# Expert outputs added into one row per token by the scatter, and the last norms' roots taken for three and for two tiles together

## The chip, the cores and the metric

The kernel runs on one core of one Trainium2 chip. Its five engines work side by side and wait for each other by semaphores: TensorE (PE; its weight loads are PEld), VectorE (DVE), ScalarE (ACT), GpSimd (POOL) and SyncE (SP), which only issues transfers. Sixteen DMA engines move the data; SyncE's transfers stand in the profile as queue q1 (hardware), GpSimd's as q0 (software). The metric is the device time of one execution in microseconds.

## The reference, cut to what matters

One trunk layer is computed for 128 context tokens and 512 latent tokens: 640 tokens of 1024 numbers, five tiles of 128 tokens. After both attentions and the first norm comes the part that the change touches:

```python
def hier_moe(h, ...):                       # 16 experts: top-1 group of 4, top-2 expert in it
    ...
    for e in range(N_EXPERTS):
        gg, uu = jnp.split(t @ w_gate_up[e], 2, axis=-1)
        out = out + combine[:, e:e + 1] * ((jax.nn.silu(gg) * uu) @ w_down[e])
    return out.reshape(b, s, d)

x = ln_affine(DEEPNORM_ALPHA * x + g2 * hier_moe(h, ...), ln2_g, ln2_b)
```

Only two of the 16 weights `combine` of a token are not zero. So there are 640 x 2 = 1280 pairs of token and expert, and each token's output is the sum of two rows. All numbers are float32, and each matmul is done in three passes over high and low parts of its operands.

## The kernel before, in words

**Order of the whole.** The kernel is one block with a program for each engine, written out by hand. The stages follow each other: projections (0 to 484 us), attention, branches and output projection with the first norm, routing, the expert loop (about 1085 to 1440 us), the last norm.

**Routing.** The pairs are laid into slots, 128 to a tile, with whole tiles for each expert; here 19 tiles are used. `words` holds three words for each pair: the row to be written (expert choice times 640 plus token), the token and the weight. VectorE forms `tile_words` (L1412 to L1415) and `at_place` (L1417), TensorE turns them into a table of slots (L1753), and VectorE writes that to `table` (L1463, L1464). A slot without a pair keeps the number 4096 (`NOBODY`), which lies above the bound of both indirect transfers, so that such a row is not moved.

**Expert loop.** For each tile, GpSimd gathers 128 rows of `h2_scr` into `xs`, TensorE turns them and computes gate, up (24 matmuls each) and down (24), ScalarE and VectorE split weights and activations in high and low parts. Weights land in three places of four chunks of 0.5 MB (`w_raw`, `raw_b`, `raw_c`). SyncE loads a chunk as soon as VectorE has split the former one in its place (`expert_in`, L760), so a chunk is issued almost a full turn of its place before it is used. ScalarE scales the output to `yo` (`take_out`, L965). GpSimd's `store_rows` then does in order: copy of the addresses and gather for tile + 3, scatter of `yo` to `pair_scr` (L1981), wait for that scatter, copy of the next addresses (L1985). When all is stored it signals `moe_over`.

**Last norm.** SyncE waits for `moe_over` and loads two rows for each token, `ya` and `yc` (L776, L777). VectorE: `combine` adds them, multiplies by the gate and adds the residual, with the row's sum (L1494 to L1498); `root_z` computes 1/sqrt of one tile's variance by `rsqrt_column` (10 small operations); `gain_z` multiplies by the gain (L1509). ScalarE: `square_z` and `norm_z`. The loop over tiles has combine, gain of two tiles before, root of the tile before. GpSimd stores each tile with a DMA that adds to the output (L2003), which SyncE set to the bias at the start (L700).

**Around the new transfers.** At about 41 us SyncE issues the bias copies, then loads projection weights block by block. After the last block before the attention (a block of `w_br_b`) it waits for the end of the projections (`pj_ready`) and then loads the second attention bundle. The first attention bundle is loaded by GpSimd, near the end of the projections, with the stores of the gate rows around it (L411 to L422, L1833).

## Time and profile before

| | us |
|---|---|
| median of 3 runs | 1500.85 (1499.09 to 1501.25) |
| the profiled execution | 1499.63 |
| its span | 1497.4 |
| TensorE busy | 1300.7 (87% of the span) |
| VectorE busy | 989.6 (66%) |
| ScalarE busy | 649.3 (43%) |
| GpSimd busy | 171.7 (11%) |

All times are microseconds from the span's start unless marked ns. "Idle before <- releaser" is the time in which the engine had nothing to do and what ended it. A share of the transfer engines is the time that packets took, over that of 16 engines; where two queues' packets overlap in time it can be a little over one. "To landing" runs from the issue of a transfer to its semaphore.

### The profile page before, as it was taken

How to read it: one execution, taken by the hardware profiler on the slowest of the kernel's cores; microseconds unless marked ns; L12 is line 12 of the kernel's file. 1: busy time of each engine (PE TensorE's matmuls, PEld its weight loads, DVE VectorE, ACT ScalarE, POOL GpSimd, SP SyncE). 2: the span in 40 equal slices, each digit the busy share in tenths (PEclk: the TensorE clock that was granted, in tenths of full speed). 3: DMA queues.
4: the chain of work that ended last, by engine and by line, in shares of the span. 5: the costliest groups of instructions: out<-in, count | busy, mean ns of one | idle time of the engine just before them, and what ended most of it. 6: DMA issues, size and time to landing. Idle time of an engine off the chain costs nothing.

```text
span 1497.4 us, 20859 instructions
## 1 busy us (share of the span) xinstructions
PE 1300.7 (87%) x6836; PEld 1063.8 (71%) x6836; DVE 989.6 (66%) x1814; ACT 649.3 (43%) x962; POOL 171.7 (11%) x236
## 2 busy tenths in 40 slices
PE   6899999999999778799986799996389999999940
PEld 3677777667887667788886688785368888888830
DVE  3655521838561777755555844499689999999936
ACT  2422222323222566545553322200357888888812
POOL 0012111111122000000000000100101121112201
PEclk9799999999999899999998799997589999999975
DMA  9856554453535676602202434436489999999834
GB/s 354 268 183 218 190 211 162 155 183 102 183 134 172 160 181 173 172 26 61 80 19 69 160 121 137 146 137 243 166 301 354 364 383 388 391 391 375 312 149 70
DMA packets 144419, 301.05 MB, mean 201 GB/s; under 512 B 18972, under 2 KB 24636, under 8 KB 144344
## 3 DMA queue, kind: packets, MB, share of 16 engines
q1 hardware_dynamic: 122104, 232.19, 45.1%
q0 software_dynamic: 20800, 62.63, 13.1%
q10 hardware_dynamic: 1440, 5.24, 1.1%
q8 instruction: 45, 0.74, 0.2%
q14 instruction: 30, 0.25, 0.1%
HBM read 258.69 MB, written 53.90 MB: 209 GB/s over the span
## 4 chain that ended last, share of the span: by engine, by line
PE 73%; DVE 14%; issue 6%; ACT 4%; DMA 2%; SPq 1%; POOL 0%; ACTq 0%; DVEq 0%; POOLq 0%
PE psum_pair L1556 7%; PE psum_pair L1557 7%; PE psum_pair L1558 7%; PE psum_pair L1777 5%; PE psum_pair L1778 5%; PE psum_pair L1779 5%; PE psum_pair L1695 4%; PE psum_pair L1643 4%; PE psum_pair L1696 4%; PE psum_pair L1697 4%; PE psum_pair L1656 4%; PE psum_pair L1633 4%; PE psum_pair L1792 2%; PE psum_pair L1793 2%; PE psum_pair L1794 2%
## 5 line engine op out<-in xcount | busy, mean ns | idle before, releaser
L1556 PE MATMUL psum_pair<-w_parts,h_hi 128*128 128x512 f32 x520 | 209.9, 404 | 6.3 <-DVE h_lo L1164 6.3
L1557 PE MATMUL psum_pair<-w_parts,h_hi 128*128 128x512 f32 x520 | 205.5, 395 | 0.0
L1558 PE MATMUL psum_pair<-w_parts,h_lo 128*128 128x512 f32 x520 | 205.4, 395 | 0.0
L1186 DVE TENSOR_REDUCE minus_max<-psum_pair 128x1 f32<-128x640 f32 (+1 forms) x160 | 114.3, 715 | 99.0 <-PE psum_pair L1633 98.6
L874 ACT ACTIVATE p_unnormed<-psum_pair,minus_max 128x640 f32<-128x640 f32 (+1 forms) x160 | 113.5, 709 | 144.4 <-DVE minus_max L1186 144.2
L1022 DVE TENSOR_TENSOR w_parts<-w_raw,w_parts 128x1024 fp32r<-128x1024 f32 x72 | 83.3, 1220 | 106.1 <-ACT w_parts L789 106.0
L1633 PE MATMUL psum_pair<-k_bundle,q_bundle 128*128 128x512 f32 (+1 forms) x576 | 128.4, 342 | 5.8 <-ACT p_unnormed L874 5.1
L1656 PE MATMUL psum_pair<-v_bundle,p_turned 128*128 128x64 f32 (+1 forms) x1008 | 131.3, 275 | 0.0
L1556 PEld LDWEIGHTS psum_pair<-w_parts,h_hi 128*128 128x128 f32 x520 | 99.2, 191 | 37.4 <-issue 18.3
L1656 PEld LDWEIGHTS psum_pair<-v_bundle,p_turned 128*128 128x128 f32 x1008 | 122.9, 193 | 1.4
L1558 PEld LDWEIGHTS psum_pair<-w_parts,h_lo 128*128 128x128 f32 x520 | 99.3, 191 | 21.5
L1557 PEld LDWEIGHTS psum_pair<-w_parts,h_hi 128*128 128x128 f32 x520 | 99.5, 191 | 19.0
L1633 PEld LDWEIGHTS psum_pair<-k_bundle,q_bundle 128*128 128x128 f32 x576 | 89.0, 195 | 13.8 <-issue 6.8
L1435 DVE TENSOR_TENSOR w_parts<-w_raw_b,w_parts 128x1024 fp32r<-128x1024 f32 x76 | 88.0, 1220 | 4.3 <-ACT w_parts L951 4.3
L1435 DVE TENSOR_TENSOR w_parts<-w_raw,w_parts 128x1024 fp32r<-128x1024 f32 x76 | 87.8, 1217 | 0.6 <-ACT w_hi_c L951 0.6
L1435 DVE TENSOR_TENSOR w_lo_c<-w_raw_c,w_hi_c 128x1024 fp32r<-128x1024 f32 x76 | 87.8, 1216 | 0.2 <-ACT w_hi_c L951 0.2
L789 ACT CAST w_parts<-w_raw 128x1024 fp32r<-128x1024 f32 x72 | 70.3, 1047 | 40.3 <-PE psum_pair L1697 38.1
L800 ACT ACTIVATE turned_staging<-psum_pair 128x1024 f32<-128x1024 f32 (+1 forms) x38 | 36.4, 960 | 108.0 <-PE psum_pair L1588 108.0
L951 ACT CAST w_hi_c<-w_raw_c 128x1024 fp32r<-128x1024 f32 x76 | 73.7, 1047 | 7.6 <-DVE control L1426 7.6
L1695 PE MATMUL psum_pair<-w_parts,oA_turned_hi 128*128 128x512 f32 x160 | 66.0, 413 | 9.4 <-DVE oA_turned_lo L1232 7.9
L951 ACT CAST w_parts<-w_raw 128x1024 fp32r<-128x1024 f32 x76 | 74.0, 1051 | 0.2 <-issue 0.2
L951 ACT CAST w_parts<-w_raw_b 128x1024 fp32r<-128x1024 f32 x76 | 73.9, 1053 | 0.0
(311 smaller groups left out, 2585.0 us busy)
## 6 DMA issues: line engine op xcount, KB each, us to landing
w_raw<-in_w_gate_up SPq DMA_DIRECT2D x76, 512.0 KB, 7.6
w_raw_c<-in_w_gate_up SPq DMA_DIRECT2D x72, 512.0 KB, 8.6
w_raw_b<-in_w_down SPq DMA_DIRECT2D x72, 512.0 KB, 7.7
w_raw<-in_w_in SPq DMA_DIRECT2D x52, 512.0 KB, 8.8
ada_raw<-in_w_ada SPq DMA_DIRECT2D x32, 512.0 KB, 7.1
k_bundle<-k_transposed SPq DMA_DIRECT2D x28, 384.0 KB, 8.2
q_transposed<-turned_staging POOLq DMA_DIRECT2D x20, 512.0 KB, 4.0
ada_raw_early<-in_w_ada SPq DMA_DIRECT2D x16, 512.0 KB, 8.2
```

What stands on the lines that cost most here:

```text
L874: act.activation(pbuf[:, m % PR, 0:w], spair(m)[:, 0:w], ACT.Exp, bias=nmax[:, m % RR:m % RR + 1], accum_out=rsum[:, m % RR:m % RR + 1]).t ...
L951: act.copy(expert_hi(place, c), landing(place, c)).then_inc(hi_done, 1)
L1022: dve.tensor_tensor(w_parts[b % 2][:, 1, c], w_raw[:, c], w_parts[b % 2][:, 0, c].bitcast(F32), ALU.subtract).then_inc(lo_done, 1)
L1186: dve.tensor_reduce(nmax[:, m % RR:m % RR + 1], spair(m)[:, 0:width(j)], AX.X, ALU.max, negate=True).then_inc(nb_done, 1)
L1435: dve.tensor_tensor(expert_lo(place, c), landing(place, c), expert_hi(place, c).bitcast(F32), ALU.subtract).then_inc(lo_done, 1)
L1556: pe.matmul(bank(n), a_hi, hi, start=first, stop=False)
L1557: pe.matmul(bank(n), a_hi, lo, start=False, stop=False)
L1558: last = pe.matmul(bank(n), a_lo, hi, start=False, stop=end)
L1633: last = pe.matmul(spair(m)[:, c0:c0 + w], q, k[:, g, k0:k0 + w], start=g == 0, stop=g == 1)
L1656: last = pe.matmul(obank(j)[:, 0:w], ptb[:, j % 2, k], vb[bi % 2][:, vt, 0:w], start=k == 0, stop=k == len(tiles) - 1)
L1695: pe.matmul(out, a_hi[:, kk], hi, start=kk == 0, stop=False)
L1777: pe.matmul(out, xt_hi[:, kk], hi, start=kk == 0, stop=False)
```

## The change

Both experts' outputs of a token are now added into one row of `sum_scr` by the scatter itself (`compute_op=ALU.add`). The rows must be zero first: SyncE writes a row of zeros to memory at the start and copies it to all 768 rows before the attention. A slot without a pair writes to one of 128 spare rows behind the 640 (row 640 + p for place p), by a minimum with `spare`, so every scatter has 128 rows within its bound. The scatters of different tiles were already waited for one by one. The words per pair go from three to two. After the loop SyncE loads five tiles instead of ten and `combine` has one operation less. The roots are computed for tiles 0 to 2 and for tiles 3 and 4 together, by `rsqrt` (two operations and three rounds of three) instead of `rsqrt_column` (two and three rounds of two), and VectorE's and ScalarE's orders are written out anew.

```diff
-        pair_scr = dram("pair_rows", (2 * NT * P, D))
+        sum_scr = dram("token_sums", ((NT + 1) * P, D))
+        zero_row = dram("zero_row", (1, D))
...
+            sp.wait_ge(cond_silu, 2)
+            sp.dma_start(zero_row[0].rearrange("(p c) -> p c", p=P), cond_cols[:, 0, 2:2 + D // P]).then_inc(zero_in, 16)
             weights(1)
             for b in range(2, NB - 4):
                 if b - 2 < N_ADA - 4:
                     ada_weights(b + 2)
                 weights(b)
+            sp.wait_ge(zero_in, 16)
+            for tt in range(NT + 1):
+                sp.dma_start(sum_scr[tt * P:(tt + 1) * P], zero_row[0:1, :].to_broadcast([P, D])).then_inc(sums_cleared, 16)
             sp.wait_ge(pj_ready, N_PJ)
...
             for tt in range(NT):
-                sp.dma_start(ya[:, tt], pair_scr[tt * P:(tt + 1) * P]).then_inc(y_in[tt], 16)
-                sp.dma_start(yc[:, tt], pair_scr[(NT + tt) * P:(NT + tt + 1) * P]).then_inc(y_in[tt], 16)
+                sp.dma_start(ya[:, tt], sum_scr[tt * P:(tt + 1) * P]).then_inc(y_in[tt], 16)
...
             def norm_z(tt):
-                act.wait_ge(zr_done, tt + 1)
+                act.wait_ge(zr_done, 1 if tt < 3 else 2)
...
-            for tt in range(NT + 1):
-                if tt < NT:
-                    square_z(tt)
-                if tt:
-                    norm_z(tt - 1)
+            for tt in range(4):
+                square_z(tt)
+            norm_z(0)
+            norm_z(1)
+            square_z(4)
+            for tt in range(2, NT):
+                norm_z(tt)
...
-                link(dve.tensor_tensor(tile_words[:, i, :, 2], over(tiles, 1, [P, NT, TILES]),
+                link(dve.tensor_tensor(tile_words[:, i, :, 1], over(tiles, 1, [P, NT, TILES]),
                                        over(place[:, 1, :, i], 2, [P, NT, TILES]), ALU.is_equal))
-                for w in range(3):
+                for w in range(2):
...
-            slot_words = pair[2][:, 0:3 * TILES].rearrange("p (w t) -> p t w", w=3)
-            dve.tensor_scalar(table[:, 0:TILES, 0:2], slot_words[:, :, 0:2], -1.0, float(NOBODY), ALU.mult, ALU.add).then_inc(table_done, 1)
-            dve.tensor_copy(table[:, 0:TILES, 2].bitcast(F32), slot_words[:, :, 2]).then_inc(table_done, 1)
+            slot_words = pair[2][:, 0:2 * TILES].rearrange("p (w t) -> p w t", w=2)
+            dve.tensor_scalar(table[:, 0:TILES, 1], slot_words[:, 0], -1.0, float(NOBODY), ALU.mult, ALU.add).then_inc(table_done, 1)
+            link(dve.tensor_copy(table[:, 0:TILES, 2].bitcast(F32), slot_words[:, 1]))
+            dve.wait_ge(table_done, 1)
+            dve.tensor_scalar(table[:, 0:TILES, 0], table[:, 0:TILES, 1], spare[:], None, ALU.min).then_inc(table_done, 1)
...
             def combine(tt):
                 y = ya[:, tt]
-                dve.wait_ge(y_in[tt], 32)
-                link(dve.tensor_tensor(y, y, yc[:, tt], ALU.add))
+                dve.wait_ge(y_in[tt], 16)
                 link(dve.tensor_tensor(y, y, g2[:, cnd], ALU.mult))
...
-            for tt in range(NT + 2):
-                if tt < NT:
-                    combine(tt)
-                if tt >= 2:
-                    gain_z(tt - 2)
-                if 1 <= tt <= NT:
-                    root_z(tt - 1)
+            for tt in range(4):
+                combine(tt)
+            root_z(slice(0, 3))
+            combine(4)
+            gain_z(0)
+            root_z(slice(3, NT))
+            for tt in range(1, NT):
+                gain_z(tt)
...
+            pool.wait_ge(sums_cleared, 16 * (NT + 1))
             pool.tensor_copy(out_now[:], table[:, 0]).then_inc(y_free, OFF)
...
-                pool.indirect_dma_start(out=pair_scr, out_offset=bass.IndirectOffsetOnAxis(ap=out_now[:, 0:1], axis=0), in_=yo[:],
-                                        in_offset=None, bounds_check=last_pair, oob_is_err=False).then_inc(y_st, 16)
+                pool.indirect_dma_start(out=sum_scr, out_offset=bass.IndirectOffsetOnAxis(ap=out_now[:, 0:1], axis=0), in_=yo[:],
+                                        in_offset=None, bounds_check=last_row, oob_is_err=True,
+                                        compute_op=ALU.add).then_inc(y_st, 16)
```

## Rows read from the trace of the kernel before

**Rows 1.** The page's strip of 40 slices (37.4 us each): transfer engines, GB/s.

```profile
DMA  9856554453535676602202434436489999999834
GB/s 354 268 183 218 190 211 162 155 183 102 183 134 172 160 181 173 172 26 61 80 19 69 160 121 137 146 137 243 166 301 354 364 383 388 391 391 375 312 149 70
```

**Rows 2.** Stretches of the expert loop: length, busy by engine, clock, DMA share, GB/s.

```profile
1120.00:1140.00 20.00, 20.00 (x94) 16.37 (x93) 18.78 (x18) 16.55 (x19) 3.75 (x5) 1.00 0.97 338
1140.00:1160.00 20.00, 20.00 (x95) 16.33 (x94) 18.81 (x19) 16.36 (x18) 2.93 (x4) 1.00 1.01 370
...
1180.00:1198.00 18.00, 18.00 (x85) 14.74 (x85) 16.82 (x16) 14.55 (x17) 3.13 (x4) 1.00 0.99 359
...
1270.00:1288.00 18.00, 18.00 (x86) 14.74 (x85) 16.82 (x16) 14.55 (x17) 3.38 (x4) 1.00 1.05 392
```

**Rows 3.** Median landing of place c's chunks, stretches 1154 to 1172 and 1334 to 1352.

```profile
w_raw_c<-in_w_gate_up SPq DMA_DIRECT2D x4, 512.0 KB, 6.0
...
w_raw_c<-in_w_gate_up SPq DMA_DIRECT2D x4, 512.0 KB, 11.9
```

**Rows 4.** Timeline, SyncE and ScalarE: issue and rounding of place c's four chunks.

```profile
1350.43 4.51 SPq L760 DMA_DIRECT2D w_raw_c<-in_w_gate_up  x4
...
1365.33 3.88 ACT L951 CAST w_hi_c<-w_raw_c 128x1024 fp32r<-128x1024 f32 x4
```

**Rows 5.** Timeline of the last norm: first operations of combine 0, 1, 2; last store.

```profile
1450.25 1.22 DVE L1494 TENSOR_TENSOR first_expert_rows<-first_expert_rows,second_expert_rows 128x1024 f32<-128x1024 f32 x1 [17.78 <-DMA second_expert_rows<-pair_rows]
...
1454.10 1.21 DVE L1494 TENSOR_TENSOR first_expert_rows<-first_expert_rows,second_expert_rows 128x1024 f32<-128x1024 f32 x1
...
1459.93 1.22 DVE L1494 TENSOR_TENSOR first_expert_rows<-first_expert_rows,second_expert_rows 128x1024 f32<-128x1024 f32 x1
...
1488.22 0.85 POOL L2003 DMA_DIRECT2D out_y_prompt<-first_expert_rows  x1 [3.66 <-DVE first_expert_rows L1509]
```

**Rows 6.** Transfers of 1478.5 to 1497 (GB/s, queue share), and landings of L2003.

```profile
GB/s 0 0 0 0 142 35 62 142 177 213 186 159 18 0 142 35 89 177 204 221 195 71 0 0 142 97 133 195 230 195 142 0 0 0 0 0 0 0 0 0
...
q0 software_dynamic: 432, 1.57, 55.8%
...
DMA to landing us min/median/max: 5.3/5.4/5.6
```

**Rows 7.** Transfers of 1445 to 1464: the ten loads after the loop.

```profile
GB/s 0 0 121 43 190 405 431 414 414 405 405 423 414 423 423 423 431 414 414 405 414 414 414 414 414 405 414 414 405 414 311 9 0 0 0 0 0 0 0 0
...
q1 hardware_dynamic: 1440, 5.24, 72.0%
```

**Rows 8.** Landings of L1981; plain stores, 1000 to 1126; last scatter's bytes and wait.

```profile
DMA to landing us min/median/max: 2.5/6.8/7.1
...
h_rows<-rows POOLq DMA_DIRECT2D x4, 512.0 KB, 2.9
...
q0 software_dynamic: 144, 0.26, 15.9%
...
1441.91 3.20 DMA pair_rows<-expert_out_rows,rows_written
```

**Rows 9.** Timeline, GpSimd: the address copy after a scatter in the loop.

```profile
1367.88 3.44 POOL L1985 COPY rows_written<-words_of_slot 128x4 uint32 x1 [5.99 <-DMA pair_rows<-expert_out_rows,rows_written]
```

**Rows 10.** Transfers of 463 to 482, by queue: packets, MB, share.

```profile
q0 software_dynamic: 830, 3.40, 68.5%
q1 hardware_dynamic: 829, 1.58, 27.4%
```

**Rows 11.** There: the bundle's last part (us to landing), and ScalarE's two last copies.

```profile
v_bundle<-in_cache_a_v POOLq DMA_DIRECT2D x1, 64.0 KB, 13.1
...
482.15 0.60 ACT L818 ACTIVATE value_staging<-psum_pair 128x512 f32<-128x512 f32 x1 [8.08 <-DMA gate_tanh<-value_staging]
484.34 0.60 ACT L818 ACTIVATE value_staging<-psum_pair 128x512 f32<-128x512 f32 x1 [1.60 <-PE psum_pair L1558]
```

**Rows 12.** Timeline, VectorE in the routing: the small multiplications.

```profile
1070.91 0.94 DVE L1415 TENSOR_TENSOR tile_words<-tile_words,words_of_pair 128x125 f32<-128x125 f32 x3
```

More of the change, by code:

```diff
@@ L439, in hybrid_step @@
         places = sb("places", [P, P], F32, s4)
+        spare = sb("spare_row", [P, 1], F32, s4)
         table = sb("words_of_slot", [P, TCOLS, 4], U32, s4)
@@ L484, in hybrid_step @@
         zn = sb("z_shift", [P, NT], F32, s7)
[L485 to L486 removed]
+        zt = sb("z_root_step", [P, NT], F32, s7)
+        zi = sb("z_root_bits", [P, NT], I32, s7)
         s7.close()
@@ L571, in hybrid_step @@
         moe_over = sem("moe_over")
+        zero_in = sem("zero_row_set")
+        sums_cleared = sem("sums_cleared")
         ln2_g, g2 = rows[:, 0], rows[:, 1:3]
@@ L1330, in _ @@
             dve.wait_ge(words_set, 4)
-            link(dve.tensor_scalar(words[:, :, :, 0:2], words[:, :, :, 0:2].bitcast(U32), -1.0, float(NOBODY), ALU.mult, ALU.add))
+            link(dve.tensor_scalar(words[:, :, :, 0], words[:, :, :, 0].bitcast(U32), -1.0, float(NOBODY), ALU.mult, ALU.add))
             link(dve.tensor_copy(places[:], places[:].bitcast(U32)))
+            link(dve.tensor_copy(spare[:], spare[:].bitcast(U32)))
             dve.wait_ge(gate1_in, 32)
@@ L1498, in combine, with root_z @@
                 dve.tensor_scalar(zm[:, tt:tt + 1], zs[:, tt:tt + 1], -1.0 / D, None, ALU.mult).then_inc(z_done, 1)
-            def root_z(tt):
-                c = slice(tt, tt + 1)
-                dve.wait_ge(zq_done, tt + 1)
+            def root_z(c):
+                n = c.stop - c.start
+                dve.wait_ge(zq_done, c.stop)
                 link(dve.tensor_scalar(zv[:, c], zq[:, c], 1.0 / D, EPS, ALU.mult, ALU.add))
-                rsqrt_column(dve, link, zr[:, c], zv[:, c], zt[:], zi[:])
+                rsqrt(dve, link, zr[:, c], zv[:, c], zt[:, 0:n], zi[:, 0:n])
                 dve.tensor_tensor(zn[:, c], zm[:, c], zr[:, c], ALU.mult).then_inc(zr_done, 1)
@@ L1752, in _ @@
                 for tt in range(NT):
-                    last = pe.matmul(pair[2][:, 0:3 * TILES], at_place[:, i, tt], tile_words[:, i, tt].rearrange("p w t -> p (w t)"),
+                    last = pe.matmul(pair[2][:, 0:2 * TILES], at_place[:, i, tt], tile_words[:, i, tt].rearrange("p w t -> p (w t)"),
                                      start=i == 0 and tt == 0, stop=i == 1 and tt == NT - 1)
@@ L1928, in _ @@
                 if v == 0:
-                    pool.iota(words[:, :, :, 0].bitcast(U32), [[NT * P, 2], [P, NT]], base=0, channel_multiplier=1).then_inc(words_set, 1)
-                    pool.iota(words[:, :, :, 1].bitcast(U32), [[0, 2], [P, NT]], base=0, channel_multiplier=1).then_inc(words_set, 1)
+                    pool.iota(spare[:].bitcast(U32), [[0, 1]], base=NT * P, channel_multiplier=1).then_inc(words_set, 1)
+                    pool.iota(words[:, :, :, 0].bitcast(U32), [[0, 2], [P, NT]], base=0, channel_multiplier=1).then_inc(words_set, 1)
                     pool.iota(places[:].bitcast(U32), [[1, P]], base=0, channel_multiplier=0).then_inc(words_set, 1)
```

12 lines of the change are left out of this document (5 added, 7 removed).

## The prediction

> **What bounds the kernel now.** I read the profile in this order: its page, the table of stretches over the expert loop, the transfers of single stretches, the timeline of the end, and the stretch ahead of the attention. The page's strip of slices shows the transfer engines at 9 tenths, and 354 to 391 GB/s, from about 1120 us to 1385 us: the expert loop [rows 1]. One iteration of that loop takes 18.0 us, in which TensorE has no gap, so TensorE sets the pace there; but in the same rows the transfer share climbs from 0.97 to 1.05 and stays at 1.05 [rows 2]. The landing times say what that means. The expert weights for landing place c need 6.0 us from issue to landing around 1160 us and 11.9 us around 1340 us [rows 3], ten iterations later. A chunk waits behind a backlog that grows by 0.6 us per iteration at up to 392 GB/s [rows 2, 3]: the transfer engines are already slightly over their capacity, and only the distance between issue and use hides it. A chunk of place c is issued at 1350.43 and rounded by ScalarE at 1365.33: 14.9 us of cover, of which 11.9 are used up. 3.0 us are left [rows 3, 4].
>
> After the loop the path is the last scatter, ten loads, then VectorE with five tiles of final norm one after the other, and the output stores [rows 5].
>
> **The change, part by part.**
>
> *The scatter adds (loop).* Before, a tile's scatter wrote only the slots that hold a pair: the reference has 640 tokens and 2 experts each, so 1280 rows of 4 KB, 5.24 MB over 19 scatters. Now an empty slot points at a spare row, so each scatter moves all 128 rows (0.524 MB), and each row is added. The trace of before has no adding scatter, but it has an adding store of the same 128 rows of 4 KB, the output store. Three of them take 55.8% of 18.5 us, 3.44 us of all 16 engines each, and their busiest slices move 177 to 230 GB/s [rows 6]. Ten plain loads of the same size take 72.0% of 19 us, 1.37 us each, at 405 to 431 GB/s [rows 7]. So an added row costs the engines 2 times (by the rate of the busy slices) to 2.5 times (by the share) a plain one. I take 2 times, 2.74 us per scatter, since in the loop another queue can fill the gaps that make up the rest; 3.44 stays as the upper end, 1.37 (the add costs nothing, only the rows are more) as the lower.
> Sixteen scatters fall while weights are still being loaded (1127 to 1397 us, one per iteration). The last of the 19 carries 0.26 MB [rows 8]; with under 0.1 MB for the two before it, which land in 2.5 and under 5 us, the sixteen move about 4.9 MB today: 4.9/0.524 x 1.37 = 12.8 us of engine time. After: 16 x 2.74 = 43.8. The difference, 31.0 us, divided by the 1.04 to 1.05 by which shares exceed one in the full stretches, is 29.8 us of work for a resource that is already full. What absorbs it: the first iterations lie below 1.05 by 0.08 of 20 us, twice 0.04 of 20 us and 0.06 of 18 us, 4.3 us together [rows 2]; and the 3 us of cover left at the end [rows 4]. 29.8 - 7.3 = **+22.5 us**. The ends: 16 x 1.37 gives 21.9 - 12.8 = 9.1, over 1.04 is 8.8, less 7.3 = +1.5; 16 x 3.44 gives +33.
> The Trainium skill, "DMA: Bandwidth & Descriptors", section on the anatomy of one DMA on the gpsimd path, fits one transfer as 2.0 us plus bytes over 436 GB/s, with no term for an add. That is 3.2 us for 0.524 MB. The trace agrees for a plain store from GpSimd (2.9 us to landing) and not for the adding one (5.3 to 5.6 us), so here the measurement decides [rows 6, 8]; taken at its word the rule gives the lower end above.
>
> The wait for the scatter itself is covered in the loop. It lands 6.8 us after its issue (median) [rows 8]; behind it on GpSimd are the copy of the next addresses, then the copy and the gather for tile +3, the first of which starts when the scatter has landed, at 1367.88, and ends at 1371.3 [rows 9]. A scatter that lands 2 to 3 us later makes the gather about that much later; its transposes are due some 9 us after the gather lands now (one 7 us transfer behind 1372.4, against 1388.4 where TensorE turns that tile). Cost 0; with transfers full this is where a second loss could start.
>
> *Clearing 768 rows.* SyncE issues six copies of 0.5 MB, memory to memory, after the block of w_br_b at 463.7 us; it next has something to issue at 487.86, so the six issues (0.6 to 0.7 us each) are free. Their transfers are not: just then GpSimd's loads of the first attention bundle and the stores of the gate rows hold the engines fully, 68.5% + 27.4% of 19 us [rows 10], and the last bundle part lands at 468.37 + 13.1 = 481.5; ScalarE waits until 482.15 for a gate store behind it [rows 11]. Six copies at 1.37 us are at least 8.2 us. With two queues served in turn between a third and all of it comes ahead of the bundle: +2.7 to +8.2, of which 2.8 us are covered, since the projections' last result is taken out at 484.34 [rows 11]. So 0 to +6, and up to +9 if copies within memory cost more than loads. I take **+3**.
>
> The 4 KB copy of zeros before `weights(1)` fits in SyncE's wait there: 0. The wait of GpSimd for the clearing is satisfied 500 us earlier: 0.
>
> *Tables.* Two of ten small multiplications of 0.31 us go (0.94 us for three now) [rows 12], and the matmuls are 50 columns for 75 (at most 0.5 us); behind them the first gather starts that much sooner. The extra `min` lies behind the word that the first gather takes. **-0.6**, between 0 and -1.2.
>
> *The end.* The last scatter landed 3.2 us after issue with half its rows [rows 8]; with 128 added rows it needs another 2.74 - 0.69 = 2.1, up to 2.7 by the share: +2.3. The first add was allowed after two loads, at 1450.25; now one suffices: -1.37. So the first `combine` starts at 1451.2. Its pitch was 3.85 us for three long operations; with two it is 3.85 - 1.24 = 2.61 [rows 5]. Four: 1461.6. The root of three columns has 13 small operations where one column's had 10 in 1.98 us (1454.10 + 3.85 = 1457.95 to 1459.93), so about 2.6: 1464.2. The fifth combine: 1466.8. ScalarE meanwhile squares and norms (1.35 and 1.25 us each) and finishes the fifth square at 1468.2. First gain at 1466.8, second root 1468.2 to 1470.8, four gains of 1.14 to 1.2: 1475.4. GpSimd issues the last store at 1475.7 instead of 1488.2: 12.5 us sooner. But the stores then come closer than they can be served: issues at 1468.2, 1472.2, 1473.4, 1474.6, 1475.7, each with 2.74 to 3.44 us of engine time. The second lands at 1472.2 + 5.3 = 1477.5, and three more at 3.0 each at 1486.5, where the last landed at 1488.2 + 5.3 = 1493.5 before. **-7.0** (-5.7 by 3.44, -7.8 by 2.74; -12.5 if stores overlapped freely).
>
> Sum: +22.5 + 3 - 0.6 - 7.0 = +17.9. On the profiled execution's 1499.63 that is 1517.5; the median of the runs is 1.2 above it: 1518.7, and I say 1518.
>
> **The rivals.**
> Faster: *the loop has room.* If an added row holds a transfer engine no longer than a plain one beside weight loads (or the backlog of rows 3 comes only from bursts), the loop costs 0 to 1.5 us, the clearing 0 to 3, and the end's -7.6 with the tables remains: 1493 to 1498, say 1495. For it: TensorE has no gap today, and the growth of landing times stops when tiles get emptier. Against it: shares of 1.05 nowhere exceeded, and a factor of 2 in rate with nothing else running. 0.16.
> Slower, more: *the add costs its full share* (3.44 us, perhaps more with HBM busy): +33 + 5 - 0.6 - 6 = +31, so 1532. For it, the 45 to 56% shares; against it, that slices between are empty. 0.12.
> *GpSimd's chain becomes the bound*: scatter, copy, gather, transposes each in turn. A scatter of 15 us instead of 7 makes the gather late by its 9 us of cover; from there every further us counts 16 times. Needs twice the landing that two times the row cost gives: 0.05, around 1535.
> *No change*: the terms cancel, in between the first rival and the forecast: 0.05.
>
> **How the numbers follow.** The forecast has 0.62, with its own range 1505 to 1528. Faster by over 0.2% (3 us, about what can be told from nothing here) 0.15; within 0.2% 0.05; slower 0.80. The range of 8 in 10 reaches down to 1500, since the first rival is the largest left out, and up to 1533.
>
> **What would show it.** In the profile after: weight landings in the loop rising to about 15 us by the fifth or sixth iteration, then ScalarE idle before the rounding of weights, waiting for them, and iterations of 19.5 to 20.5 us; scatter rows landing at 8 to 10 us; q0's share near 20% of the loop. The first attention exponent a few us after 486.9. At the end, VectorE's last gain about 24 us after the first combine (37.5 us before), and output stores that land at 3 us intervals, later than their issue by up to 11 us. Iterations that stay at 18.0 us make the forecast wrong by its largest term; a landing that stays below 14 us says that an added row costs less than twice.

## The result, and the profile after

The changed kernel takes 1515.6 us (median of 4 runs, 1514.66 to 1518.03) against 1500.47 us for the kernel before (4 runs, 1499.09 to 1501.25): a ratio of 1.0104, 95% interval 1.0087 to 1.0122. It is slower by 15 us, or 1%. The forecast was 1518 with a range of 1500 to 1533. The profiled execution took 1514.66 us, with a span of 1512.8 us.

The page of the changed kernel, its two strips of the transfer engines, against [rows 1]:

```profile
DMA  9856554543537676602202434436589999999954
GB/s 351 264 181 216 194 203 160 172 170 101 178 129 245 152 181 176 174 19 71 80 18 69 155 121 137 153 138 229 184 316 365 367 368 367 365 364 363 356 144 103
```

What counts here: the nines of the expert loop remain (slices 31 to 38), but the rate in them is 356 to 368 GB/s where it was 383 to 391 in the fullest slices before. Engines that are just as full move less. The same over the loop, in stretches of 80 us (columns as in [rows 2]):

```profile
1120.00:1200.00 80.00, 80.00 (x376) 65.54 (x375) 74.40 (x72) 64.24 (x71) 19.95 (x18) 1.00 1.01 348
1200.00:1280.00 80.00, 77.87 (x360) 62.87 (x360) 69.68 (x66) 61.81 (x67) 16.11 (x16) 1.00 1.05 369
1280.00:1360.00 80.00, 74.74 (x341) 59.46 (x340) 69.01 (x66) 60.09 (x64) 15.24 (x16) 1.00 1.05 366
1360.00:1440.00 80.00, 75.81 (x345) 60.34 (x344) 69.61 (x66) 62.53 (x68) 14.92 (x16) 1.00 1.04 360
```

TensorE, with no gap in the rows of before, stays busy for the first 80 us and then loses 2 to 5 us in every 80. The waits of the loop (engine and line, what it waited for: us in total, times, longest) name the reason:

```profile
ACT w_hi_c L959 <- DMA w_raw_c<-in_w_gate_up: 35.8, 26, 3.1
DVE w_lo_c L1446 <- ACT w_hi_c L959: 26.1, 16, 2.3
...
ACT w_parts L959 <- DMA w_raw<-in_w_gate_up: 10.9, 23, 1.8
```

ScalarE's rounding (L959, L951 before) waits for weight chunks, most for those of place c, whose cover [rows 4] has run out. The times of waiting overlap with each other and with buffered work, so their sum is no loss of time; the loss is read from the distances between the scatters, below.

I cut both profiled executions at the same six events and took differences. "Exponent" is the start of the first attention exponent, "router" the end of the stage before the routing (last write of `h_turned`); the other columns are lengths. "End" runs from the first `combine` to the end of the span. All kernels of the experiments stand here, so that each can be read against the row of before:

```
us                     exponent  router  to 1st   loop: 1st  to first  end
                                         scatter  to 19th    combine
before                  486.9    1051.8   75.2     314.9      8.3      47.2
the change              494.1    1061.2   72.5     330.0     10.0      39.1
e1 clear later          488.8    1053.9   72.1     330.1     10.3      39.2
e2 filled rows only     492.3    1057.6   72.5     325.3      9.9      38.9
e3 all rows, no add     493.5    1058.9   72.4     314.9      7.2      38.3
e4 norm order alone     488.6    1053.6   75.0     314.9      8.4      44.1
e5 before, spread       490.0    1055.0   75.0     314.9      8.2      47.1
e6 = e2, spread, later  488.1    1052.4   71.9     321.8     10.2      37.4
e7 the change, spread   492.1    1057.4   72.3     328.8     10.0      37.6
e8 split delayed        488.4    1052.6   72.4     314.9      8.5      47.2
e9 order, delay, plain  486.4    1053.2   72.9     314.9      8.4      44.4
e10 = e6, plain stores  486.4    1051.5   71.9     321.9     10.1      38.0
e11 = e3, stored twice  494.0    1059.5   72.6     332.5      8.7      38.5
```

In e11, which has two scatters for a tile, the first of the two is counted. The change is +9.3 up to the router's end, -2.7 in the routing, +15.1 in the loop, +1.7 and -8.0 at the end: +15.4 of span. The last four columns repeat within some tenths between kernels that have the same code there. The first two don't: without the clearing in its place the exponent starts anywhere from 486.4 to 490.0, so what is said of that part from one execution is good to 2 us.

**The clearing.** Transfers of 463 to 482 us in the changed kernel, against [rows 10, 11] (packets, MB, share of the 16 engines; then KB each and median us to landing):

```profile
q1 hardware_dynamic: 1404, 3.62, 62.1%
q0 software_dynamic: 552, 2.53, 39.2%
...
token_sums<-zero_row SPq DMA_DIRECT2D x6, 512.0 KB, 17.7
...
gate_tanh<-value_staging POOLq DMA_DIRECT2D x3, 256.0 KB, 16.2
...
v_bundle<-in_cache_a_v POOLq DMA_DIRECT2D x1, 64.0 KB, 19.6
```

The queue of GpSimd has 39.2% where it had 68.5%, and the last part of the bundle lands after 19.6 us instead of 13.1. ScalarE's last copies of that stage, and the first exponent:

```profile
489.56 0.60 ACT L826 ACTIVATE value_staging<-psum_pair 128x512 f32<-128x512 f32 x1 [15.21 <-DMA gate_tanh<-value_staging]
...
494.13 0.80 ACT L882 ACTIVATE p_unnormed<-psum_pair,minus_max 128x640 f32<-128x640 f32 x1 [2.47 <-DVE minus_max L1196]
```

The copy that started at 482.15 starts at 489.56: 7.4 us, the wait for the gate store 15.21 instead of 8.08. The Trainium skill, "DMA: Bandwidth & Descriptors", section "SWDGE vs HWDGE vs iDMA", has each transfer engine go round its queues in turn. The trace agrees: the two queues, 39.2% and 62.1%, share the engines, and neither is served first. TensorE waits behind that copy, and the stretches of 5 us show its clock beside it:

```profile
485.00:490.00 5.00, 0.00 (x0) 0.00 (x0) 0.00 (x0) 0.45 (x1) 0.00 (x0) 0.80 0.65 240
490.00:495.00 5.00, 2.82 (x8) 2.13 (x8) 1.67 (x4) 1.72 (x5) 1.08 (x2) 0.50 0.30 112
495.00:500.00 5.00, 4.20 (x12) 3.17 (x12) 3.07 (x6) 2.67 (x7) 0.00 (x0) 0.50 0.87 226
```

TensorE does nothing for 5 us, and then runs at a granted clock of 0.50, the lower of its two levels (1.2 GHz; the upper is 2.4). The kernel before, over the same times, was busy for 3.68 us in the first stretch, had 0.53 in the second and 0.81 in the third:

```profile
485.00:490.00 5.00, 3.68 (x15) 3.03 (x16) 2.42 (x5) 1.70 (x5) 0.54 (x1) 0.79 0.31 81
490.00:495.00 5.00, 4.35 (x17) 3.34 (x16) 3.10 (x6) 2.66 (x6) 0.00 (x0) 0.53 1.05 286
495.00:500.00 5.00, 3.18 (x18) 2.71 (x17) 3.13 (x6) 2.35 (x5) 0.00 (x0) 0.81 0.99 210
```

So the low clock is there without the gap too. It is back at 1.00 from 505 us in the kernel before and from 510 us in the change, 18 and 16 us after their first exponents, and no price of it can be read from this.

**The end.** VectorE in the changed kernel, against [rows 5]: the first combine, the second, the last group of gains; then the last output store:

```profile
1473.69 1.23 DVE L1507 TENSOR_TENSOR first_expert_rows<-first_expert_rows,rows 128x1024 f32<-128x1024 f32 x1 [18.24 <-DMA first_expert_rows<-token_sums]
...
1476.29 1.22 DVE L1507 TENSOR_TENSOR first_expert_rows<-first_expert_rows,rows 128x1024 f32<-128x1024 f32 x1
...
1492.94 4.62 DVE L1521 TENSOR_TENSOR first_expert_rows<-second_expert_rows,rows 128x1024 f32<-128x1024 f32 x4
...
1498.11 0.85 POOL L2018 DMA_DIRECT2D out_y_prompt<-first_expert_rows  x1 [0.53 <-DVE first_expert_rows L1521]
```

The pitch is 2.60 us (forecast 2.61) and the last store is issued 24.4 us after the first combine (forecast 24.5; 38.0 before). The transfers from 1487 us to the end show what the other 5.5 us of these 13.6 turned into:

```profile
GB/s 0 0 0 0 0 0 0 0 102 19 203 203 203 127 108 140 121 210 197 178 152 216 197 203 203 210 216 203 210 203 178 32 25 6 0 0 0 0 0 0
...
q0 software_dynamic: 720, 2.62, 59.2%
...
out_y_sample<-first_expert_rows POOLq DMA_DIRECT2D x4, 512.0 KB, 6.9
out_y_prompt<-first_expert_rows POOLq DMA_DIRECT2D x1, 512.0 KB, 10.9
```

After the first there is no gap between the stores, at 203 to 216 GB/s in most slices, and the last lands 10.9 us after its issue, where each needed 5.3 to 5.6 before [rows 6].

### The profile page after: what moved, and what is told of

It is laid out like the page before. It is cut to its first block, busy times and chain, and to the rows that moved or that the text cites. A ratio compares the mean times of both kernels' runs of the same rounds, so it can differ in the third digit from the quotient of the medians.

```text
span 1512.8 us, 20833 instructions
## 1 busy us (share of the span) xinstructions
PE 1305.5 (86%) x6836; PEld 1063.1 (70%) x6836; DVE 982.2 (65%) x1785; ACT 655.3 (43%) x962; POOL 179.3 (12%) x236
## 3 DMA queue, kind: packets, MB, share of 16 engines
q0 software_dynamic: 20800, 67.35, 15.2%
## 4 chain that ended last, share of the span: by engine, by line
PE 56%; DVE 14%; DMA 8%; SPq 8%; issue 8%; ACT 4%; POOL 0%; ACTq 0%; DVEq 0%; POOLq 0%
PE psum_pair L1569 7%; PE psum_pair L1570 6%; PE psum_pair L1571 6%; SPq L769 6%; DMA w_raw_c<-in_w_gate_up 5%; PE psum_pair L1656 4%; PE psum_pair L1708 4%; PE psum_pair L1710 4%; PE psum_pair L1709 4%; PE psum_pair L1669 4%; PE psum_pair L1646 4%; ACT p_turned L405 2%; DVE minus_max L1196 2%; PE psum_pair L1790 2%; PE psum_pair L1791 2%
## 5 line engine op out<-in xcount | busy, mean ns | idle before, releaser
L1569 PEld LDWEIGHTS psum_pair<-w_parts,h_hi 128*128 128x128 f32 x520 | 99.2, 191 | 37.4 <-issue 18.4
L959 ACT CAST w_hi_c<-w_raw_c 128x1024 fp32r<-128x1024 f32 x76 | 77.6, 1048 | 46.5 <-DMA w_raw_c<-in_w_gate_up 35.8
L808 ACT ACTIVATE turned_staging<-psum_pair 128x1024 f32<-128x1024 f32 (+1 forms) x38 | 36.4, 960 | 107.7 <-PE psum_pair L1601 107.7
L959 ACT CAST w_parts<-w_raw 128x1024 fp32r<-128x1024 f32 x76 | 76.6, 1051 | 11.2 <-DMA w_raw<-in_w_gate_up 10.9
L959 ACT CAST w_parts<-w_raw_b 128x1024 fp32r<-128x1024 f32 x76 | 76.4, 1054 | 6.3 <-DMA w_raw_b<-in_w_down 4.4
L1708 PE MATMUL psum_pair<-w_parts,oA_turned_hi 128*128 128x512 f32 x160 | 65.9, 412 | 10.5 <-DVE oA_turned_lo L1242 8.9
```

The source lines that it names most:

```text
L959: act.copy(expert_hi(place, c), landing(place, c)).then_inc(hi_done, 1)
L1569: pe.matmul(bank(n), a_hi, hi, start=first, stop=False)
L1708: pe.matmul(out, a_hi[:, kk], hi, start=kk == 0, stop=False)
```

## The experiments

Ratios are to the kernel before, run beside them on the same chip (medians there 1499.68 for e1 to e4, 1500.72 for e5 to e8, 1499.38 for e9 to e11).

**e1, clearing later.** Only the place of the six copies moves.

```diff
-            sp.wait_ge(zero_in, 16)
-            for tt in range(NT + 1):
-                sp.dma_start(sum_scr[tt * P:(tt + 1) * P], zero_row[0:1, :].to_broadcast([P, D])).then_inc(sums_cleared, 16)
...
+            sp.wait_ge(zero_in, 16)
+            for tt in range(NT + 1):
+                sp.dma_start(sum_scr[tt * P:(tt + 1) * P], zero_row[0:1, :].to_broadcast([P, D])).then_inc(sums_cleared, 16)
             for b in range(NB - 4, NB):
                 weights(b)
```

> The six clearing copies of the changed kernel are issued after the last attention bundle's loads instead of ahead of the attention; nothing else differs. Theory (the copies delay the gate store and the bundle, and TensorE then stands and comes back at half its clock): the first attention exponent returns from 494.1 to about 487.2 us, and everything behind by about 9 us: 1506.5. Rival (the late start only moves idle time that the attention has anyway): the exponent returns, but the end by less than 4 us: 1512 or more.

Measured: 1507.54 us, ratio 1.0048 (1.0031 to 1.0065), against 1.0104: the place of the clearing alone is worth 7 to 8 us by the medians and ratios of these two kernels, near the 9 us of the theory. The copy and the exponent come back:

```profile
484.54 0.60 ACT L826 ACTIVATE value_staging<-psum_pair 128x512 f32<-128x512 f32 x1 [8.53 <-DMA gate_tanh<-value_staging]
...
488.82 0.80 ACT L882 ACTIVATE p_unnormed<-psum_pair,minus_max 128x640 f32<-128x640 f32 x1 [1.84 <-DVE minus_max L1196]
```

The exponent is 5.3 us earlier, the router's end 7.3; the loop is unchanged (330.1). All kernels of the table together say a little less. Five have the clearing in its place (the change, e2, e3, e7, e11), and their router ends at 1058.9 us in the mean, from 1057.4 to 1061.2; in the eight others it ends at 1053.0, from 1051.5 to 1055.0. That is 5.9 us, and the profiled execution of the change lies at the upper edge.

**e2, only filled rows are added.** Empty slots are skipped by the bounds check, as before the change.

```diff
-            dve.tensor_scalar(table[:, 0:TILES, 0], table[:, 0:TILES, 1], spare[:], None, ALU.min).then_inc(table_done, 1)
+            dve.tensor_copy(table[:, 0:TILES, 0], table[:, 0:TILES, 1]).then_inc(table_done, 1)
...
-                                        in_offset=None, bounds_check=last_row, oob_is_err=True,
+                                        in_offset=None, bounds_check=last_row, oob_is_err=False,
```

> The changed kernel, but an empty slot keeps the number 4096 and its row is dropped as before, so the scatters add only the 1280 rows that hold a pair. Threshold theory (the loop loses only what exceeds a cover of about 13 us of transfer-engine time): sixteen scatters add 1205 rows x 0.16 us / 16 = 12 us of engine time, which the cover still takes: iterations stay near 18.0 us and the loop loses 0 to 1 us, total 1499 to 1501. Rival (each us of added engine time costs about half a us throughout, since the loop loses 15 us for 30 added): the loop loses 6 us, total 1506. Rival (the add costs by itself, whatever the rows): near 1512.

Measured: 1507.18 us, 1.0056 (1.0039 to 1.0073); the loop is 325.3, that is +10.4. The threshold theory (a loss of 0 to 1 us) fell, and the loss lies above the 6 us of the first rival too. The empty rows account for the smaller part of the loop's loss, 4.7 of 15.1 us.

**e3, all rows, no add.** The scatter copies instead of adding, so the output lacks the sum over the two experts.

```diff
-                                        in_offset=None, bounds_check=last_row, oob_is_err=True,
-                                        compute_op=ALU.add).then_inc(y_st, 16)
+                                        in_offset=None, bounds_check=last_row, oob_is_err=True).then_inc(y_st, 16)
```

> The changed kernel with scatters that copy instead of add, all 128 rows of each tile (the sum over the two experts is left out of the computation by this). Threshold theory: 16 x 128 rows instead of 1205 are 9 us of engine time more than before, under the cover: loop 0 to 1 us, total 1498 to 1500. Rival (half a us for each us): loop 4 to 5 us, total 1504. Rival (the empty rows are the cause and the add is free): as slow as the change, 1515.

Measured: 1493.36 us, 0.9959 (0.9945 to 0.9974). The loop is 314.9, exactly that of before, with every one of the 128 rows moved. The row count alone costs nothing; something about the add does.

**e11, every row stored twice, no add.** This asks whether that something is the engine time or the add itself: two plain scatters of a tile, the second into another scratch tensor. The output lacks the sum here too.

```diff
+                pool.indirect_dma_start(out=copy_scr, out_offset=bass.IndirectOffsetOnAxis(ap=out_now[:, 0:1], axis=0), in_=yo[:],
+                                        in_offset=None, bounds_check=last_row, oob_is_err=True).then_inc(y_st, 16)
-                pool.wait_ge(y_st, 16 * (tile + 1))
+                pool.wait_ge(y_st, 32 * (tile + 1))
```

> The e3 run (all 128 rows of a tile stored plain, the sum over a token's two experts left out), but each tile is stored twice, by a second plain scatter into another scratch tensor: the DMA engines get about as much extra work as the adding scatter brought (its landing takes about twice a plain one). Theory A (what costs the loop is engine time, whatever it is spent on): the loop grows from 314.9 to 325 to 330 us, with the waits for w_raw_c as in the changed kernel, and the time is about 1503 to 1509 us. Theory B (it is the add itself, which blocks more than its own engine time): the loop stays within 3 us of 314.9, and the time is about 1494 to 1497 us. The second scatter's issue costs GpSimd about 1 us a tile, which is not on the path before the last tile.

Measured: 1511.66 us, 1.0081 (1.0066 to 1.0097); the loop is 332.5, +17.6, somewhat more than theory A's 325 to 330 us. Theory A holds against B, and nothing special to the add is needed. The waits are those of the changed kernel:

```profile
ACT w_hi_c L960 <- DMA w_raw_c<-in_w_gate_up: 38.7, 35, 2.8
```

One rival of the forecast is not told apart by e11 alone, that GpSimd's chain (scatter, copy, gather) became the bound: with two scatters the second lands 8.9 us after the issue of the first, as late as one adding scatter (8.8). The waits settle it. From the first to the last scatter no engine waits for gathered rows, in the change and in e11; and e2, whose scatters land after 8.6 us, loses 4.7 us less than the change. The landing of a scatter holds up another engine once, ahead of the last tile of the change:

```profile
ACT expert_out_rows L973 <- POOL rows_written L2000: 7.0, 1, 7.0
```

The clearest reading of the loop is one stretch, 1200 to 1400 us, of each kernel: TensorE's busy time is the second number, the share of the transfer engines and the rate are the last two; under each, the two queues (q1 carries the weights, q0 GpSimd's gathers and scatters). The kernel before:

```profile
1200.00:1400.00 200.00, 200.00 (x934) 163.86 (x933) 186.79 (x179) 162.02 (x179) 43.75 (x44) 1.00 1.04 386
...
q1 hardware_dynamic: 35821, 69.05, 93.4%
q0 software_dynamic: 3168, 8.14, 10.5%
```

The changed kernel:

```profile
1200.00:1400.00 200.00, 190.60 (x872) 152.58 (x872) 173.60 (x164) 152.95 (x164) 38.75 (x40) 1.00 1.05 367
...
q1 hardware_dynamic: 33247, 64.09, 86.4%
q0 software_dynamic: 3024, 9.25, 18.5%
```

e11, and then e3:

```profile
1200.00:1400.00 200.00, 189.32 (x866) 151.26 (x865) 172.98 (x164) 151.58 (x163) 43.96 (x50) 1.00 1.04 391
...
q0 software_dynamic: 4464, 14.49, 18.2%
```

```profile
1200.00:1400.00 200.00, 200.00 (x935) 163.88 (x934) 187.33 (x178) 161.85 (x178) 42.17 (x44) 1.00 1.04 390
...
q0 software_dynamic: 3272, 9.90, 12.6%
```

q0 holds 18.5% of the engines with 9.25 MB of which a part is added, and 18.2% with 14.49 MB of plain rows; TensorE loses 9.4 and 10.7 us. The rates differ, 367 and 391 GB/s, and don't matter. The total is 1.04 to 1.05 in all four. By q0's share the kernels fall into one order, but for the last three, which lie close together:

```
                 before  e3     e6     e2     e11    e7     the change
q0, % of engines  10.5   12.6   15.8   16.0   18.2   18.3   18.5
TensorE idle, us   0      0      3.6    5.5   10.7    9.1    9.4
```

**e5, e6 and e7: rows spread over the engines.** In the kernel before, the rows of a half-filled tile are the first ones of the 128. I suspected that the 16 engines then have unequal shares, and that the fullest sets the landing.

```diff
-                    pool.iota(places[:].bitcast(U32), [[1, P]], base=0, channel_multiplier=0).then_inc(words_set, 1)
+                    pool.iota(places[:].bitcast(U32).rearrange("p (a b) -> p a b", a=16), [[1, 16], [16, 8]], base=0, channel_multiplier=0).then_inc(words_set, 1)
```

> The kernel before, with only the places of a tile renumbered: the r-th slot of a tile lies on partition 8 (r mod 16) + r div 16 instead of r, so the filled rows of a half-full tile are spread over the sixteen transfer engines (each serves 8 neighbouring partitions). Theory (the filled rows used to lie on the first engines, each with 8 rows per gather and per scatter however empty the tile; the fullest engine sets the pace of the weights): landings of place c rise much less, from 6 to at most 8 us instead of 11.9, while iterations stay at 18.0 us and the total is that of before, 1499, or 1 less. Rival (all engines are loaded alike already): landings rise to 11 or 12 as before.

> The changed kernel with three edits: the clearing copies after the attention's loads, empty slots dropped, and the slots spread over the partitions. Theory (the fullest engine): a scatter of 67 rows on average now costs each engine 4.2 x 0.33 us, as much as the fullest one paid before, so the loop loses nothing (18.0 us per iteration, 314.9 us from first to last scatter); with the tables' 2.7, the end's 7 to 8 gained and the clearing away: 1490. Rival (an adding scatter costs the loop by its issue or its landing, whatever the engines): the loop keeps the 10.4 us that the version with dropped rows lost: 1500.

> The changed kernel with only the slots spread over the partitions; the scatters still add all 128 rows. Theory (fullest engine): the scatter loads all engines alike already, only the gathers get evener, by 8 x 0.165 x 0.47 = 0.6 us per iteration: the loop loses about 8 us instead of 15.1, total 1508. Rival (spreading helps by something else, such as which memory is written): as fast as the version with dropped rows. Rival (mean load counts): 1515.6 as before the edit.

Measured: e5 (before, spread) 1499.98 us, 0.9994 (0.9984 to 1.0004), landings of place c about 11.1 us near the end of the loop where 11.9 stood [rows 3]. e7 (the change, spread) 1510.43 us, 1.0067 (1.005 to 1.0084), loop 328.8, 1.2 shorter. e6 (e2 with the spread and the later clearing) 1495.7 us, 0.997 (0.9956 to 0.9984), loop 321.8, 3.4 shorter than e2's. So the theory fell in its main claim: it had the landings at 8 us at most in e5, no loss in e6's loop (it is 6.9) and a loss of 8 us in e7's (it is 13.9). The spread brings 1 to 3 us where rows are added and nothing that can be told where they are plain. Why it brings more in e6 than in e7 stays open.

**e4, the norm order alone.** The kernel before with the change's order of the last norms, and pair rows as before. ScalarE's order and the roots for three and two tiles go with it as in the change.

```diff
-            for tt in range(NT + 2):
-                if tt < NT:
-                    combine(tt)
-                if tt >= 2:
-                    gain_z(tt - 2)
-                if 1 <= tt <= NT:
-                    root_z(tt - 1)
+            for tt in range(4):
+                combine(tt)
+            root_z(slice(0, 3))
+            combine(4)
+            gain_z(0)
+            root_z(slice(3, NT))
+            for tt in range(1, NT):
+                gain_z(tt)
```

> The kernel before with only the new order of the last norm: roots for three and for two tiles by rsqrt, still ten loads and the addition of both rows. VectorE would issue the last store about 8 us sooner (1480.4 instead of 1488.2). Theory (adding output stores are served one after the other, 3.2 us each by the profile of the changed kernel): first lands at about 1478.7, last at 1491.5, so 2 us gained: 1498.5. Rival (stores overlap): all 8 us gained, 1492.5.

Measured: 1497.65 us, 0.9979 (0.997 to 0.9989). The last store is issued 30.5 us after the first combine instead of 38.0, but the end shrinks by only 3.0, since the stores now stand in line:

```profile
L2006 POOL DMA_DIRECT2D out_y_prompt<-first_expert_rows x1: 850/850/850, 1482.3 to 1482.3; - x1
...
DMA to landing us min/median/max: 9.8/9.8/9.8
```

**e8, VectorE's split delayed.** The routing fell by 2.7 us and my terms explain 0.6. The traces differ in one more thing: in the changed kernel VectorE starts its first split of weights after GpSimd has issued the first gather's transfer. Before:

```profile
1078.28 4.63 DVE L1435 TENSOR_TENSOR w_parts<-w_raw,w_parts 128x1024 fp32r<-128x1024 f32 x4 [0.62 <-ACT w_hi_c L951]
1078.59 1.88 POOL L1963 DMA_INDIRECT expert_in<-h_rows,words_of_slot  x1 [23.44 <-DVE words_of_slot L1464]
...
1084.17 1.97 PE L1763 MATMUL psum_pair<-identity,expert_in 128*128 128x128 f32 x8 [6.87 <-DMA expert_in<-h_rows,words_of_slot]
```

The changed kernel:

```profile
1087.33 1.09 POOL L1976 DMA_INDIRECT expert_in<-h_rows,words_of_slot  x1 [22.79 <-DVE words_of_slot L1477]
1087.64 4.69 DVE L1446 TENSOR_TENSOR w_parts<-w_raw,w_parts 128x1024 fp32r<-128x1024 f32 x4 [0.70 <-issue]
...
1090.67 1.54 PE L1776 MATMUL psum_pair<-identity,expert_in 128*128 128x128 f32 x6 [4.34 <-DMA expert_in<-h_rows,words_of_slot]
```

From the issue to TensorE's turn it is 5.58 us before and 3.34 after. e8 does this alone, with three small writes to an unused column ahead of VectorE's last copy:

```diff
+            for _ in range(3):
+                link(dve.memset(table[:, 1:TILES, 3], 0))
             dve.tensor_copy(table[:, 0:TILES, 2].bitcast(F32), slot_words[:, :, 2]).then_inc(table_done, 1)
```

> The kernel before with three tiny writes of VectorE (an unused word of the table) ahead of its last table copy, so that its first splitting of expert weights starts about 0.5 us later, behind the issue of the first gather. Theory (that split and the weight loads it releases slow the gather): the gather's issue takes 1.1 instead of 1.9 us, its rows are there 3.3 instead of 5.6 us later, and the stretch from the last turned row of the router to the first scatter shrinks from 75.2 to about 73.1 us. Rival (the smaller table does it): 75.2 plus the 0.5 us of the writes.

```profile
1079.35 1.09 POOL L1965 DMA_INDIRECT expert_in<-h_rows,words_of_slot  x1 [23.46 <-DVE words_of_slot L1466]
1079.68 4.68 DVE L1435 TENSOR_TENSOR w_parts<-w_raw,w_parts 128x1024 fp32r<-128x1024 f32 x4 [0.74 <-issue]
```

The issue takes 1.09 us instead of 1.88, and the way to the first scatter 72.4 us instead of 75.2, with more instructions than before. The kernel ran once, in 1497.58 us. The table bears the reading out: the way is 75.0 to 75.2 us in the three kernels with the old order (before, e4, e5) and 71.9 to 72.9 in the ten others. The rows come 2.2 us sooner, of which the issue is 0.8; what makes the rest, the weight loads that the split releases or something else, is not told apart.

The Trainium skill, "SBUF — State Buffer", section "Who interferes with whom", says that a VectorE instruction with two inputs in SBUF contends with a GpSimd instruction that reads SBUF, and that a probe saw such an operation not stall the issue of a transfer. The split is one (`w_raw` and `w_parts`), and the gather reads its addresses from SBUF. The trace agrees with the first half: 0.8 us more of issue. It does not agree with the second for this indirect gather.

**e9 and e10, candidates with plain output stores.** e9 is the kernel before with the order of e4 and the delay of e8, e10 is e6; in both the final stores are plain, VectorE adds the bias, which is loaded once near the end, and the five early stores of the bias are left out.

```diff
-                dve.tensor_tensor(ya[:, tt], yc[:, tt], ln2_g, ALU.mult).then_inc(zg_done, 1)
+                link(dve.tensor_tensor(ya[:, tt], yc[:, tt], ln2_g, ALU.mult))
+                dve.wait_ge(out_cleared, 16)
+                dve.tensor_tensor(ya[:, tt], ya[:, tt], xq[0], ALU.add).then_inc(zg_done, 1)
...
-                pool.dma_start(dst, ya[:, tt], accum_op=ALU.add).then_inc(out_st, 16)
+                pool.dma_start(dst, ya[:, tt]).then_inc(out_st, 16)
```

> The kernel before with three things joined: the norm order of the e4 run, VectorE's split put 0.6 us later as in the e8 run, and plain output stores. For these the bias is loaded once at the end, VectorE adds it (1.25 us a tile), and the five early stores that fill the output with the bias are left out. Theory (the adding stores are served one after another at 5.3 us each, so they and not VectorE end the kernel): VectorE's last store issue moves from 30.5 to 36.7 us after the first combine, a plain store needs 2.9 us, and the stretch from first combine to end falls from 44.1 to 41 us: 1497.65 - 2.8 (routing) - 3 = about 1492 us. Rival (stores were overlapped, VectorE is the end): the stretch grows by the 6 us of adds to about 48 to 50, and the time is about 1500 us.

> The e6 run (scatter that adds, filled rows alone, spread over the engines, clearing later) with the same plain output stores and one bias load. By the same theory its stretch from first combine to end falls from 37.4 to about 35 us (VectorE's last issue 24.4 + 6.2, then 4.4), loop and routing stay as in e6: 1495.7 - 2.4 = about 1493 us. Rival: 1500 us or more, as the adds lengthen VectorE's work at the end. Against e9 it tells whether the saved loads at the end (about 6 us) outweigh the loop's stall (6.9 us): within 2 us of each other.

Measured: e9 1494.53 us, 0.9967 (0.9955 to 0.9979), e10 1495.66 us, 0.9979 (0.9968 to 0.9991). Both beat the two kernels of this case, e9 by 5 us over before and 20 over the change. But the plain stores have no part in it: the end is 44.4 us in e9 (e4: 44.1) and 38.0 in e10 (e6: 37.4). In e9:

```profile
L2008 POOL DMA_DIRECT2D out_y_prompt<-first_expert_rows x1: 532/532/532, 1485.8 to 1485.8; - x1
...
DMA to landing us min/median/max: 2.9/2.9/2.9
```

The stores do land in 2.9 us, with no queue, and the last is issued 36.5 us after the first combine, as forecast. I had allowed 1.5 us from the landing to the end of the span; it is 5.0 (1488.7 to 1493.7), and was 3.9 in e4 (1482.3 + 9.8 = 1492.1 to 1496.0). VectorE's five adds took the place of the queue, one for one. So the expected fall of the end to 41 us (e9) and 35 us (e10) did not come. That e9 is at before - 5 agrees with e4 (-2) and e8 (-3, one run) together.

## Why the prediction was right, step by step

**What bounds the loop: right.** The forecast had the transfer engines over their capacity, a cover of a few us, and after that TensorE waiting behind ScalarE's rounding. The waits and the order by q0's share show it, and e11 reproduces the loss without any add. The alternative that an added row costs the engines no more than a plain one is excluded by the 18.5% on 9.25 MB, where e3 has 12.6% on 9.90.

**The size of the loop's term: +22.5 forecast, +15.1 measured.** The working can be redone from the 200 us stretches. An iteration loads 12 chunks of 0.524 MB, 6.29 MB. Weights cost 93.4% x 200 / 69.05 = 2.71 us per MB before and 86.4% x 200 / 64.09 = 2.70 after, so 17.0 us an iteration in both. q0 costs 10.5% x 200 = 21.0 us in 69.05/6.29 = 10.98 iterations before, 1.91 us each, and 37.0 us in 10.19 after, 3.63 each. The change adds 1.72 us per iteration, where the forecast had 31.0/16 = 1.94. The "2 times a plain row" was right: from e3 to e11 (2.33 to 3.59 us) a second plain scatter adds 1.26 us, the gather is then 1.07, and the adding scatter 3.63 - 1.07 = 2.56 us, 2.03 times a plain one. What was too dear is the plain row, 1.37 us a tile by the loads after the loop. Then 17.0 + 3.63 = 20.6 us of engine time, at a share of 1.05, is 19.6 us; that this equals 200/10.19 is no check, since both come from the same counts. The distances between scatters are one, with 19.7 us in the mean from the sixth to the sixteenth (us):

```
before      17.6  18.0 (x15)  17.1  9.8
the change  17.6  18.0 18.0 18.0 18.0 19.5 21.2 18.6 21.3 18.3 19.7 21.2 18.5 20.1 18.5 19.9 15.0 8.6
```

The stall starts with the sixth distance, and the lag reaches about 18.5 us after the sixteenth. With the measured cost, 16 x 1.72 / 1.05 = 26.2, less the 7.3 us that the forecast let the first iterations and the cover absorb, is 18.9. So the absorption was right, and the engine time was 3.6 us too high. Another 3.4 us come back at the end: the last two distances are 15.0 and 8.6 instead of 17.1 and 9.8. The forecast had no term for this. In the last one the same 24 matmuls take less time at a higher clock, before and after:

```profile
1432.08:1441.91 9.83, 7.36 (x24) 5.56 (x24) 0.38 (x1) 1.11 (x1) 1.17 (x2) 0.83 0.02 5
...
1455.09:1463.67 8.58, 5.74 (x24) 4.43 (x24) 0.37 (x1) 1.11 (x1) 1.80 (x2) 1.00 0.39 61
```

It is 1.00 and 8.5 to 8.6 us in e1 and e7 as well, and 0.82 or 0.83 and 9.7 to 9.9 us in e2, e3 and e11. Why the distance ahead of it shrinks by 2 us stays open.

The other kernels check that sum, each with what its own last two distances give back. e3 adds 25.2/10.83 - 1.91 = 0.42 us per iteration, 6.4 in sixteen over 1.05, and loses nothing: below the 7.3 of cover. e2 adds 32.0/10.16 - 1.91 = 1.24, so 18.9, less 7.3, less 2.0 (its last two are 15.1 and 9.9): 9.6, with 10.4 measured. e11 adds 36.4/10.14 - 1.91 = 1.68, so 25.6, less 7.3, less 2.1 (15.2 and 9.7): 16.2, with 17.6 measured. The same for e6 (64.80 MB of weights) gives 8.2 with 6.9 measured, and for e7 (64.07 MB) 14.7 with 13.9. The sum holds to 1.4 us in all of them.

One of the forecast's signs was wrong: a landing of place c below 14 us was to say that an added row costs less than twice a plain one. The profile gives none for the change, but in e7, with the same scatters, the median from 1200 to 1400 us is 13.5, and the factor is 2.

**The clearing: +3 forecast, 0 to +9 as its bounds, 5 to 9 measured; mis-sized, the other way.** The mechanism was the one described: six copies between the bundle's parts, landing of the last part 6.5 us later. The term took a middle of the bounds with 2.8 us of them covered; no cover is seen: ScalarE's copy starts 7.4 us later and the exponent 7.3. In the profiled change the delay then grows from 7.3 to 9.3 us by the router's end. That is not the price of a slower TensorE: from exponent to router it takes 567.1 us there, but 565.3 to 565.4 in e2, e3, e7 and e11, which have the same copies in the same place and the same clock of 0.50 behind them, and 565.0 in the kernel before.

**The tables: -0.6 forecast, -2.7 measured.** The gain came from something that the diff doesn't show: VectorE's split now starts a few tenths behind the gather's issue instead of ahead of it. e8 gets 2.8 us from that alone, with the larger tables, so for the removed operations, less the added `min`, nothing is left that these rows could show.

**The end: -7.0 forecast, -6.3 measured.** The pitch, the last issue and the line of stores came out as worked. The first combine started 1.7 us later relative to the last scatter, instead of 0.9.

The total was nearer than its parts. In the profiled execution the loop was over by 7.4 us, and the stretch with the clearing came out 6.3 longer and the tables 2.1 shorter than forecast: two misses of opposite sign cancelled. That the total was off by only 2.4 us is luck to that extent; the direction and the largest term were not.

## What to carry to other kernels

Where transfer engines are full, a change is priced in their time, not in bytes or rates: one queue's share of the engines in a stretch, over the iterations in it, gives the price of a step before and after, and the cover that is left says from which point it counts. An operation on rows in memory that saves loads at the end is paid for in every iteration of such a loop. A transfer that nobody waits for still needs a place in the trace where the engines are free: the same six copies cost 5 to 9 us in one place and nothing that could be seen in another.

## What the runs showed of the hardware

- Added rows cost the transfer engines what plain rows of twice the number do: q0 at 18.5% with 9.25 MB (added scatters and plain gathers) and 18.2% with 14.49 MB all plain; by the differences between the kernels, 2.56 us of all engines for 128 added rows of 4 KB and 1.26 for plain ones. Stores of 0.5 MB with add move 203 to 216 GB/s alone, plain ones land in 2.9 us.
- GpSimd's issue of an adding scatter takes 1.6 us, of a plain one 1.01; the second plain one of e11 took 1.41 (medians).
- GpSimd's issue of a gather takes 1.88 us when VectorE's long operation starts 0.3 us before it, 1.09 when it starts 0.3 us after, and the rows come 2.2 us sooner counted from the issue.
- The same 24 matmuls of the last tile kept TensorE busy for 7.36 us at a granted clock of 0.83 and for 5.74 us at 1.00.
- TensorE ran at a granted clock of 0.50 behind 5 us in which it did nothing, and at 0.53 in the kernel before without such a gap. From the first exponent to the router's end it then took 565.3 to 565.4 us in four of the five kernels with the clearing ahead of the attention (567.1 in the fifth) and 565.0 in the kernel before.
